# Output projections whose second half goes token tile by token tile, with the following norm and router work ordered by tile

## What is computed

```python
# layer 0
x = x + g1 * (attention(modulate(rmsnorm(x), s1, sc1) @ w_qkv) @ w_o)
x = x + g2 * swiglu(modulate(rmsnorm(x), s2, sc2))            # 2816 hidden
# layer 1
x = x + g1 * (fourier_mix(modulate(rmsnorm(x), s1, sc1)) @ w_f)
x = x + g2 * top2_of_8_experts(modulate(rmsnorm(x), s2, sc2)) # router: softmax(h @ w_router)
y = rmsnorm(x)
# s, sc, g: rows of silu(cond) @ ada_w + ada_b, two conditions (prompt, sample), six groups a layer
```

## Time and profile before

| | |
|---|---|
| median of the runs | 1403.02 us (1400.78 to 1403.23) |
| the profiled execution, its own time | 1397.1 us |
| its span, first to last instruction | 1395.3 us |
| granted TensorE clock, mean | 0.985 |
| TensorE busy | 1350.1 us (97%) |
| chain that ended last | TensorE 89%, GpSimd 4%, VectorE 3%, ScalarE 1% |
| experts' stage | about 621 us to 1380 us |
| dense SwiGLU | about 244 us to 517 us |

### The profile page before, as it was taken

One profiled execution on the slowest core, in us unless ns is written; L12 is line 12 of the kernel. 1 busy time (PEld: TensorE's weight loads), 2 busy tenths in 40 slices (PEclk: granted clock), 3 DMA queues, 4 the chain that ended last, 5 costly groups with the idle time before them and its releaser, 6 DMA issues.

```text
span 1395.3 us, 17342 instructions
## 1 busy us (share of the span) xinstructions
PE 1350.1 (97%) x6861; PEld 1125.2 (81%) x6861; DVE 1126.7 (81%) x1043; ACT 814.0 (58%) x821; POOL 244.5 (18%) x334
## 2 busy tenths in 40 slices
PE   5999999999999999989999999999999999999995
PEld 4887566999999986788888888888888888888884
DVE  2697867476776655568999999999999999999997
ACT  4532765233232314265777777777777777777772
POOL 3000681000000023002999100000000000000101
PEclk8999999999999999989999999999999999999998
DMA  9968446755445457448899999999999999999991
GB/s 318 356 226 298 155 145 232 278 182 178 162 147 182 147 186 241 167 145 324 298 406 385 372 411 347 398 391 360 413 376 369 411 349 398 393 354 410 368 413 58
DMA packets 122199, 409.76 MB, mean 294 GB/s; under 512 B 8337, under 2 KB 39234, under 8 KB 105218
## 3 DMA queue, kind: packets, MB, share of 16 engines
q1 hardware_dynamic: 114464, 382.24, 72.9%
q0 software_dynamic: 6576, 23.14, 5.3%
q10 hardware_dynamic: 1074, 3.23, 0.6%
HBM read 398.58 MB, written 9.99 MB: 293 GB/s over the span
## 4 chain that ended last, share of the span: by engine, by line
PE 89%; POOL 4%; DVE 3%; ACT 1%; SPq 1%; issue 1%; DMA 1%; POOLq 0%; ACTq 0%; DVEq 0%
PE ps L1877 27%; PE ps L1879 27%; PE ps L1878 27%; PE ps L2308 1%; POOL xn L746 1%; POOL o_rstd L744 1%; DMA raw<-in_w_qkv 1%; PE ps L2210 1%; SPq L520 1%; PE ps L1889 1%; DVE ring_lo L1674 1%; POOL o_msq L742 1%; PE ps L2152 1%; PE ps L2282 1%; PE ps L2231 0%
## 5 line engine op out<-in xcount | busy, mean ns | idle before, releaser
L1674 DVE TENSOR_TENSOR ring_lo<-raw,ring_hi 128x2048 fp32r<-128x2048 f32 (+1 forms) x210 | 450.4, 2167 | 35.2 <-ACT ring_hi L1102 35.1
L1102 ACT ACTIVATE ring_hi<-raw 128x2048 fp32r<-128x2048 f32 (+1 forms) x210 | 381.4, 1820 | 122.6 <-PE ps L1879 112.2
L1877 PE MATMUL ps<-ring_hi,xe 128*128 128x512 f32 x536 | 211.7, 395 | 2.0 <-DVE xe L1734 1.2
L1878 PE MATMUL ps<-ring_hi,xe 128*128 128x512 f32 x536 | 209.3, 390 | 0.0
L1879 PE MATMUL ps<-ring_lo,xe 128*128 128x512 f32 x536 | 209.3, 390 | 0.0
L845 ACT ACTIVATE ring_hi<-raw 128x2048 fp32r<-128x2048 f32 x52 | 99.1, 1912 | 152.8 <-PE ps L1879 141.0
L1246 DVE TENSOR_TENSOR ring_lo<-raw,ring_hi 128x2048 fp32r<-128x2048 f32 x52 | 118.1, 2287 | 74.7 <-ACT ring_hi L845 74.5
L1674 DVE TENSOR_TENSOR ring_lo_more<-raw,ring_hi_more 128x2048 fp32r<-128x2048 f32 (+1 forms) x70 | 151.6, 2166 | 12.6 <-ACT ring_hi_more L1102 12.6
L1102 ACT ACTIVATE ring_hi_more<-raw 128x2048 fp32r<-128x2048 f32 (+1 forms) x70 | 127.4, 1820 | 39.0 <-PE ps L1879 36.1
L1877 PEld LDWEIGHTS ps<-ring_hi,xe 128*128 128x128 f32 x536 | 101.1, 189 | 22.7 <-DVE xe L1734 1.6
L1879 PEld LDWEIGHTS ps<-ring_lo,xe 128*128 128x128 f32 x536 | 101.0, 188 | 21.2
(11 more groups left out here) (332 smaller groups left out, 2446.6 us busy)
## 6 DMA issues: line engine op xcount, KB each, us to landing
raw<-in_w_gu_e SPq DMA_DIRECT2D x128, 1024.0 KB, 8.9
raw<-in_w_down_e SPq DMA_DIRECT2D x88, 1024.0 KB, 9.3
raw<-in_w_gu_e SPq DMA_DIRECT2D x64, 768.0 KB, 7.1
raw<-in_ada_w SPq DMA_DIRECT2D x40, 1024.0 KB, 5.5
raw<-in_w_gu SPq DMA_DIRECT2D x44, 512.0 KB, 4.8
raw<-in_w_qkv SPq DMA_DIRECT2D x12, 1024.0 KB, 9.6
raw<-in_w_down SPq DMA_DIRECT2D x11, 1024.0 KB, 5.0
raw<-in_ada_w SPq DMA_DIRECT2D x16, 512.0 KB, 11.4
```

What stands on the lines that cost most here:

```text
L1102: act.activation(ehi[m % RINGM][:, 0:w], raw[:, (MOE_U0 + m) % RAW, 0:w], ACT.Copy).then_inc(hi_ready, 1)
L1674: dve.tensor_tensor(elo[m % RINGM][:, 0:w], raw[:, (MOE_U0 + m) % RAW, 0:w], ehi[m % RINGM][:, 0:w].bitcast(F32), ALU.subtract).then_inc(l ...
L1877: pe.matmul(out, l_hi, r_hi, start=first, stop=False)
L1878: pe.matmul(out, l_lo, r_hi, start=False, stop=False)
```

## The change

1. The second output half of both projections: for each tile both units one after the other, so that a tile is finished after 24 matmuls in a row. TensorE waits for both units' low parts at tile 0, and both units are released in the last tile. Tile 0 of the norm is turned between tiles 1 and 2.
2. ScalarE and VectorE do addition, square, scale, modulation and high part tile by tile in a new order (`by_tiles`, `norm_scale`, `norm_tile`).
3. `split_hi(FFN0 + 1)` and `split_lo(FFN0 + 1)` come behind the norm on their engines. `STREAM` and SyncE's program are as before. TensorE: tile 1 turned, `ada_unit(3, 0)` to `(3, 2)`, tile 2 turned, `ada_unit(3, 3)` to `(3, 5)`.
4. The router's products per tile: logits of tile 0 and two `turn_back` come ahead of the turning of tile 2. The first expert unit's low part `lo(0)` comes behind `select(0)`, its neighbour `hi(1)` behind the rows' copies.
5. At the start ScalarE keeps and modulates tile 2 ahead of `split_hi(1)`, and VectorE makes the low part of unit 1 in four pieces behind the columns of quarter 1; TensorE waits piece by piece.

```diff
@@ scalar @@
+            def by_tiles(n, turned, split):
+                high = (lambda k: high_part(n, split, k)) if split is not None else (lambda k: None)
+                square(n, 0)
+                scaled(n, 0)
+                square(n, 1)
+                modulate_tile(n, turned, 0)
+                scaled(n, 1)
+                high(0)
+                square(n, 2)
+                modulate_tile(n, turned, 1)
+                high(1)
+                modulate_tile(n, turned, 2)
+                high(2)
...
-            keep_turned(1)
-            first_modulate(0, 1)
-            split_hi(QKV0 + 1)
-            keep_turned(2)
-            first_modulate(0, 2)
+            for k in (1, 2):
+                keep_turned(k)
+                first_modulate(0, k)
             for q in range(1, MODS):
-                if q > 1:
-                    split_hi(QKV0 + q)
+                split_hi(QKV0 + q)
...
-            for s in range(WO0 + 2, FFN0 + 2):
+            for s in range(WO0 + 2, FFN0 + 1):
                 split_hi(s)
             act.wait_ge(ctx_stored, 32)
-            norm_rows(1)
-            modulate(1, 2, MODS + TURNS)
+            by_tiles(1, 2, MODS + TURNS)
+            split_hi(FFN0 + 1)
...
-            norm_rows(3)
-            modulate(3, 4, None)
-            for m in range(RING - 1):
-                hi(m)
+            by_tiles(3, 4, None)
+            hi(0)
...
+            hi(1)
@@ vector @@
             split_lo(FFN0)
+            dve.wait_ge(ctx_stored, 32)
+            add_projection(0, 1, WO0, (0, 1))
+            norm_scale(1)
+            norm_tile(1, 2, 0)
+            add_projection(0, 1, WO0, (2,))
+            norm_tile(1, 2, 1)
+            scale_last(1)
+            low = low_parts(MODS + TURNS)
+            low(0)
+            norm_tile(1, 2, 2)
+            low(1)
+            low(2)
             split_lo(FFN0 + 1)
-            add_projection(0, 1, WO0)
-            dve.wait_ge(ctx_stored, 32)
-            norm_dve(1, 2, MODS + TURNS)
...
-            add_projection(1, 1, WF0)
-            norm_dve(3, 4, None)
+            add_projection(1, 1, WF0, (0, 1))
+            norm_scale(3)
+            norm_tile(3, 4, 0)
+            add_projection(1, 1, WF0, (2,))
+            norm_tile(3, 4, 1)
+            scale_last(3)
+            norm_tile(3, 4, 2)
...
-            lo(0)
...
             select(0)
+            lo(0)
@@ tensor @@
+                for k in range(TILES):
+                    for s in (2, 3):
+                        if k == 0:
+                            pe.wait_ge(lo_ready, first + s + 1)
...
+                        if k == TILES - 1:
+                            ins.then_inc(unit_used, 1)
+                    if k < 2:
+                        ins.then_inc(proj_acc, 1)
+                    after_tile(3, k)
...
+                if (s, k) == (3, 1):
+                    turn_tile(1, 0)
             projection(WO0, 0, hlo_ready, 3 * MODS, upper_heads)
-            turn_normed(1, lambda k: ada_unit(3, k) if k < 2 else None)
-            for k in range(2, KC - 2):
+            turn_tile(1, 1)
+            for k in range(3):
+                ada_unit(3, k)
+            turn_tile(1, 2)
+            for k in range(3, KC - 2):
                 ada_unit(3, k)
...
+            turn_tile(3, 1)
+            logits(0)
+            turn_back(0)
+            turn_back(1)
+            turn_tile(3, 2)
+            logits(1)
+            logits(2)
+            for n in range(2, 2 * TILES):
                 turn_back(n)
```

More of the change, by code:

```diff
@@ L851, in norm_rows @@
             def norm_rows(n):
[L853 to L868, removed]
+                square(n, 0)
[3 more added lines that the diff above has]
+                scaled(n, 1)
+            def square(n, k):
+                x_ready(n, k)
+                act.activation(xn[:, k, :], x[:, k, :], ACT.Square,
+                               accum_out=ssq[:, n, k:k + 1]).then_inc(ssq_ready, 1)
@@ L870, in modulate, with scaled, modulate_tile @@
+            def scaled(n, k):
+                act.wait_ge(rstd_ready, 3 * n + k + 1)
+                act.activation(xn[:, k, :], x[:, k, :], ACT.Copy, scale=rstd[:, n, k:k + 1]).then_inc(xn_ready, 1)
+            def modulate_tile(n, turned, k):
                 gs, vs = NORMS[n][0:2]
                 act.wait_ge(mod_a_ready, n + MODS)
[L872 to L881, removed]
@@ L882, in modulate @@
-                if split is not None and behind:
-                    high_part(n, split, TILES - 1)
+                act.wait_ge(xT_ps, 3 * (turned + TURNS) + k + 1)
+                for q in range(4, KC):
+                    ins = act.activation(h32[:, q, k * P:(k + 1) * P],
+                                         ps[:, 2 * k + 1, (q - 4) * P:(q - 3) * P], ACT.Identity,
+                                         scale=mod_a[:, n, q, COND[k]:COND[k] + 1],
+                                         bias=modv[:, gs, vs, q, COND[k]:COND[k] + 1])
@@ L1364, in first_norm @@
                                       modv[:, 0, 0, kc, COND[k]:COND[k] + 1], ALU.mult, ALU.add).then_inc(h32_ready, 1)
-                    if (q, k) == (0, 0):
-                        first_split_lo(0)
-                        first_low(0, 0)
+                    if q < 2 and k == 0:
+                        first_split_lo(q, 0)
+                        first_low(q, 0)
                         for part in (1, 2, 3):
[L1369 to L1373, removed]
+                            first_split_lo(q, part)
+                        if q == 0:
+                            scale_last(0)
+                    elif q < 2 and k == 1:
+                        first_low(q, 1)
+                    elif q > 1 and k:
                         first_low(q, k - 1)
@@ L1382, in low_parts, with norm_scale @@
                 return low
-            def norm_dve(n, turned, split):
+            def norm_scale(n):
                 gs, vs, gc, vc, row = NORMS[n]
@@ L1391, in norm_dve, with norm_tile @@
                 dve.wait_ge(mod_a_ready, n + MODS)
[L1392 to L1405, removed]
+            def norm_tile(n, turned, k):
+                gs, vs = NORMS[n][0:2]
+                dve.wait_ge(xT_ps, 3 * (turned + TURNS) + k + 1)
+                for q in range(4):
+                    ins = dve.tensor_scalar(h32[:, q, k * P:(k + 1) * P],
+                                            ps[:, 2 * k, q * P:(q + 1) * P],
+                                            mod_a[:, n, q, COND[k]:COND[k] + 1],
+                                            modv[:, gs, vs, q, COND[k]:COND[k] + 1], ALU.mult, ALU.add)
+                ins.then_inc(h32_ready, 1)
             first_norm(0)
@@ L1544, in _, with add_projection @@
                 low_heads(1, k)
-            def add_projection(w, n, first):
-                for k in range(TILES):
+            def add_projection(w, n, first, tiles=range(TILES)):
+                for k in tiles:
                     if k < 2:
@@ L1630, in _ @@
                 add_gated(yacc, n)
-            norm_dve(2, 3, None)
+            norm_scale(2)
+            norm_tile(2, 3, 0)
+            scale_last(2)
+            norm_tile(2, 3, 1)
+            norm_tile(2, 3, 2)
             for k in range(TILES):
@@ L2244, in _, with logits @@
             projection(WF0, 1, None, 0, between_tiles)
-            turn_normed(3)
             pe.wait_ge(route_loaded, 48)
-            for k in range(TILES):
+            def logits(k):
                 pe.wait_ge(h32_ready, 3 * (MODS + 2) + k + 1)
@@ L2261, in turn_back @@
                 ins.then_inc(tokT_ps, 1)
-            for n in range(2 * TILES):
+            turn_tile(3, 1)
[6 more added lines that the diff above has]
+            for n in range(2, 2 * TILES):
                 turn_back(n)
```

58 lines of the change are left out of this document (38 added, 20 removed).

## The result

The changed kernel takes **1404.6 us** (14 runs, 1402.0 to 1406.2) against 1400.1 us for the kernel before (14 runs, 1398.3 to 1403.7) measured beside it: a ratio of 1.0029, 95% interval [1.0022, 1.0037], so 4.1 us slower. Two later comparisons gave 1.0055 [1.0037, 1.0074], or 7.7 us, and 1.0041 [1.0027, 1.0055], or 5.7 us. All runs of the study together have medians of 1404.8 (27 runs) and 1399.9 us (92 runs), 4.9 us apart. Forecast were +7.0 us and 1410.0 us. The forecast time was 5.4 us too high: 3.0 us of that lie in the level of the kernel before, the rest in the difference.

What follows compares the result with a forecast made beforehand. It took TensorE, busy 1350 of 1395 us, as the bound; +10.1 (norm after attention), -3.1 (before the experts) and 0 (start) gave +7.0 us, put on the median 1403.0: 1410.0 us, range 1404.5 to 1415.

Steps and rivals of the forecast that it cites:

- The refill behind the late low part: Norm after attention: `ada(3,5)` waits for the late low part, so the SwiGLU starts at 252.3, not 244.2: +8.1 us.
- The clock after the stall: Behind the stall before the SwiGLU, TensorE runs at a lower granted clock: +2.0 us, chosen between 1.5 and 3.35.
- The order by tiles: Norm after attention: the new order alone ends the last high part at 242.2 instead of 244.2: -2.0 us.
- Before the experts: Second projection's norm and router: logits and choice of rows come earlier: -3.1 us, bounds -5.0 to 0.
- the row choice at 609.8 + 8 or so: Sign in the router's stage: the choice of rows would start at about this time in us.
- The start: Second quarter's weights: 3.16 us of idleness go, but TensorE then waits for a load: 0, bounds -1.4 to +0.5 us.
- The sum: Whole kernel: +10.1 - 3.1 + 0 = +7.0 us against the profiled execution, giving 1404.1 us.
- I put the difference on the median: 1410.0 us: Whole kernel, last step: +7.0 us added to the shown runs' median, 1403.0, 5.9 us above the profiled execution.
- A: Rival before the SwiGLU: the refill isn't waited for, so the order gives -5.1 us, 1397.9; chance 0.07.
- B: Rival, whole kernel: refill waited for but given back at experts and start, no lower clock: +1.5, 1404.5 us; chance 0.08.
- D: Rival at the SwiGLU: loads behind `ada(3,5)` come one unit too late, some 3 us more, 1413 us; chance 0.05.
- C: Rival before the experts: small products and transposes keep the clock low, -3.1 becomes about -0.5: +9.6, 1412.6 us; chance 0.12.

Runs made afterwards that it cites:

- a4_after: The changed kernel without an edit, measured and profiled a third time against the kernel before: 1406.1 us, ratio 1.0041.
- e2: The kernel before with only the late split of `FFN0 + 1` behind the norm after attention: 1412.7 us, ratio 1.0100.
- e4: The kernel before with only the change's attention part (order by tiles and late split), start and router as before: 1409.8 us, ratio 1.0072.
- e6: The changed kernel with `FFN0 + 1` split inside the norm, VectorE's low part behind the last tile's addition: 1395.8 us, ratio 0.9967.
- e7: The changed kernel with `FFN0 + 1` split inside the norm, low part behind `scale_last`, `ada_unit(3, 5)` behind the second SwiGLU unit: 1395.4 us twice, ratios 0.9962 and 0.9976.
- e8: e7 with the second quarter's weights at the start split in one go as before: 1395.5 us, ratio 0.9972 to the kernel before.
- e1: The changed kernel with `ada_unit(3, 5)` moved behind the second SwiGLU unit, nothing else: 1404.6 us, ratio 1.0038.
- e0_before_again: The kernel before, unchanged, for a second profile; the three new profiled executions of it took 1400.2, 1399.9 and 1399.2 us.
- e3: The kernel before with only the change's part at the start, the second quarter's weights in pieces: 1400.6 us, ratio 1.0005.

## Why the prediction was right in direction and wrong in size

- **The refill behind the late low part** (+8.1 us, order included): right. Forecast were the last high part at 242.2, the low part's end at 246.4, landing at 251.3, the SwiGLU at 252.3; measured 242.5, 246.7, 251.5, 253.4. One reading in it was wrong: the load was taken at 4.9 us "since the queue is then empty as in the shorter one", but in the trace of before no packet was in flight at the issue of the longer one (5.4 us) either. The load took 4.8 us here and 5.0 to 5.2 in the other three profiles. Measured from the wait for `v` the SwiGLU starts 9.0 us later than before (55.54 against 46.58), of which 1.0 is the `ada` unit at the low clock.
- **The clock after the stall** (+2.0): right; 1.0 us in that `ada` unit and 1.0 in the first SwiGLU unit. Together +10.0 against +10.1 forecast, and +10.1 to +10.7 in the other three profiles. The 2.0 was a choice between 1.5 and 3.35, so that it fits this well is partly luck; a4_after has 2.6.
- **The order by tiles** (-2.0): half right. It is there in the chain (242.5 against 244.2), and e2 is slower than e4 (above), but once the stall is gone (e6, e7) nothing of it reaches the end of S2.
- **Before the experts** (-3.1): right like against like. Good profile against good profile 61.49 - 58.45 = 3.0, bad against bad 63.1 - 60.1 = 3.0. Choice of rows after the wait at 560 us: 52.85 before, 49.81 after. Only half of the 3.0 is waiting: by the rows of S3 above TensorE's idle time falls from 4.75 to 3.32 us, and the same 311 matmuls take 55.13 instead of 56.74 us at a granted clock of 0.94 for 0.92. The prediction had the second half inside its price of 0.11 us for a logit product and didn't name it. Its sign "the row choice at 609.8 + 8 or so" left out 2 us of its own +10.1: it came at 620.2.
- **The start** (0): right within what the runs can see; 1.0005 [0.9996, 1.0014] alone, and e8 within 0.2 us of e7. The idleness was ended by the DMA, as said.
- **The sum** (1397.1 + 7.0 = 1404.1 us): the four profiled executions of after took 1403.4 to 1406.7. That it comes so near is partly luck: its base was 2.8 us below the usual 1399.9, and its difference was larger than the 5.5 us by which the profiled executions differ.
- **The step that failed** is the last: "I put the difference on the median: 1410.0 us". Its two halves were both too large. The level: 1403.0 was the median of three runs, where the 14 runs beside the change have 1400.1 and all 92 have 1399.9, so 5.9 us were added to the profiled execution for 2.8 to 3.0. The difference: +7.0, where the medians are 4.5 us apart (4.1 by the ratio). Of that the traces show 1.5 us: the execution behind the sum had unusually little low clock in S1 and S3, stretches next to the places of the change, 3.1 us less than the other three profiles of before, and three of four profiles of after have it as low. So the terms for S1 and S3 came to -0.8 and -3.8 on average for 0 and -3.1. With four profiles of each kernel it stays open how much of this is chance. Open too is the last 1 us: the three comparisons have 4.1, 7.7 and 5.7 us, and by the second alone +7.0 would stand.

Of the rivals, A (refill not waited for) is refuted by the 9.9 us. B (given back elsewhere) had 1404.5 us, which is nearly what was measured, but by chance: it put its difference on 1403.0 too, and it needed no lower clock behind the stall, -5.0 us before the experts and -1.4 us at the start, where the runs show 2.0 us of clock, -3.0 to -3.8 us and, with the start alone, no gain (+0.7 us, interval -0.6 to +2.0). D's mechanism, loads that come too late for the SwiGLU, is real but only without the first stall (e1). C said that transposes between the small products would keep the clock low longer: low are 3.4 us at 614.0 and 3.4 at 620.8, before 6.7 at 602.9 and 3.4 at 613.2, so it was less, not more. The rule of the Trainium skill behind C ("TensorE: Matmul & The Clock Gate", Part 4, transposes don't count as busy) isn't borne out as a price here. It isn't refuted either: the prediction held against it that the clock was full up to 602.9 us behind the transposes, which is so only in some executions; in e0_before_again the sixteen transposes before the logits took 3.62 us, in before's first profile 1.97. The Trainium skill's page "TensorE: Matmul & The Clock Gate", Part 1, has another sentence that is near the failed step, that at a kernel's start the number of slow matmuls differs from run to run of one kernel; the profiles of before show the like in its middle, with 1.5 us each in S1 and S3.

## What to carry to other kernels

When a split or copy is moved later, ask first which buffer it frees and what the in-order load queue holds behind that release: here moving 4.2 us of work behind a norm delayed the loads behind that release and cost 10 us, and putting it inside the same norm, ScalarE's half where it stood idle, gave all of that back. Moving the consumer of the first late load (e1) only moved the stall. Before the terms of a profile are put on a median, take two or three profiles of the same kernel, compare the stretches next to the change, and don't take the level from three runs.

## What the runs showed of the hardware that was not expected

- The same program has a granted clock of 1.00 or 0.97 over the 53 us behind a wait of 1.4 us at 144 us, and 0.92 or 0.89 over the router's stage; each is worth 1.5 to 1.6 us, as much as the smaller terms of this sum. The two go together: in 14 of the 17 profiles of all kernels here both stretches are long or both short (S3 with the new order 60.1 or 58.4 us; not in e1, e3 and e7), so their terms don't average out within one execution.
- A stall of 9.9 us of TensorE cost 2.0 us of clock on top of it (2.6 in a4_after), not much more than the 1.5 us at least that the one of 3.16 us had cost.
- The load of 1 MB took 4.8 us from issue to landing, and 4.9 to 5.2 us in the other runs in which it was issued late, each time with nothing issued by SyncE ahead of it for several us; the two rows of before have 4.7 and 5.4, so one row was good to some tenths of a us only.
